# The position bias of the compressed keys and the latent products in the selector stage of a two-block transformer kernel

## What is computed

```python
# compressed keys (i=0) and values (i=1): blocks of 32 tokens, every 16, a learned position pe added to each
blocks = k[:, idx] + pe[:, None, :]
flat   = ....reshape(b, g, n_cmp, CMP_LEN * dh)          # 31 blocks, 2048 long
hid    = jax.nn.gelu(flat @ w1 + b1);  kc = hid @ w2 + b2
p_c    = softmax(q @ kc * scale)                          # per head: 512 x 31
# latent attention: keys and values per head from one latent row of 128 per token
sc     = (q_lat @ c_kv + q_rope @ k_rope) * scale ;  o = (p @ c_kv) @ w_uv
```

## Time and profile before

| | |
|---|---|
| median of 3 runs | 2381.52 us (2379.24 to 2383.43) |
| the profiled execution | 2381.52 us, span 2379.7 us |
| TensorE busy | 2275.6 us, 96% of the span |
| VectorE busy | 1028.7 us, 43% |
| ScalarE busy | 492.4 us, 21% |
| the stage `selector` | 232.7 to 350.4 us: 117.7 us |
| in it: TensorE, VectorE, ScalarE busy | 111.0, 96.7, 43.0 us |

### The profile page before, as it was taken

How to read it: one execution, slowest core, us unless ns; L and a number is a source line. 1 busy time by engine, 2 the same in 40 slices (tenths; PEclk the granted TensorE clock), 3 DMA queues, 4 the chain that set the end, 5 groups by cost and what they waited for, 6 DMA issues and landing times. The chain is left out here.

```text
span 2379.7 us, 26551 instructions
## 1 busy us (share of the span) xinstructions
PE 2275.6 (96%) x10439; PEld 1760.2 (74%) x10439; DVE 1028.7 (43%) x1931; ACT 492.4 (21%) x1131; POOL 687.0 (29%) x549
## 2 busy tenths in 40 slices
PE   7999988999999999999899999997999899999998
PEld 3454666677757888888778888884556568888887
DVE  4546965453335742254544223542623422111354
ACT  3101332223433000010400011112133532000002
POOL 0000000000010655565255555520010104555652
PEclk9999899899999999999999999998999999999999
DMA  9543334544431454222334432230122122232230
GB/s 322 181 134 103 112 107 142 177 155 112 106 103 39 149 185 127 81 77 73 106 125 159 142 95 70 77 110 31 36 76 71 36 71 71 71 106 60 74 97 36
DMA packets 255288, 250.14 MB, mean 105 GB/s; under 512 B 19875, under 2 KB 207421, under 8 KB 255037
## 3 DMA queue, kind: packets, MB, share of 16 engines
q1 hardware_dynamic: 254728, 248.30, 33.1%
q10 hardware_dynamic: 436, 0.15, 0.0%
HBM read 243.19 MB, written 4.19 MB: 104 GB/s over the span
## 5 line engine op out<-in xcount | busy, mean ns | idle before, releaser
L1985 POOL TENSOR_TENSOR w_sums<-ring 128x512 f32<-128x512 f32 x66 | 90.8, 1376 | 515.5 <-POOLq L1316 334.3
L2011 POOL TENSOR_TENSOR hidden<-rstd,h_act 128x256 f32<-128x256 f32 x66 | 53.8, 816 | 401.8 <-DVE h_act L2187 401.8
L1870 PE MATMUL ps<-h_sums,w_sums 128*128 128x256 f32 x528 | 128.4, 384 | 6.5 <-DVE h_sums L2123 6.1
L2187 DVE TENSOR_TENSOR h_act<-ps,rstd 128x256 f32<-128x256 f32 x78 | 33.1, 424 | 232.5 <-PE ps L1888 135.9
L814 PE MATMUL ps<-h_act,ring 128*128 128x512 f32 (+1 forms) x288 | 128.3, 600 | 5.2 <-PEq L333 4.4
L1888 PE MATMUL ps<-h_sums,ring 128*128 128x256 f32 x528 | 125.8, 381 | 3.1 <-DVE rstd L2166 3.0
L1876 PE MATMUL ps<-h_act,ring 128*128 128x256 f32 x528 | 126.4, 383 | 0.0
L1882 PE MATMUL ps<-h_sums,w_sums 128*128 128x256 f32 x528 | 125.0, 380 | 1.0 <-DVE rstd L2159 1.0
L1836 PE MATMUL ps<-h_act,ring 128*128 128x256 f32 x528 | 125.3, 381 | 0.0
L1893 PE MATMUL ps<-h_act,w_sums 128*128 128x256 f32 x528 | 124.8, 379 | 0.0
L1844 PE MATMUL ps<-h_act,ring 128*128 128x256 f32 x528 | 124.5, 380 | 0.0
(11 more groups left out here) (465 smaller groups left out, 4453.2 us busy)
## 6 DMA issues: line engine op xcount, KB each, us to landing
ring<-in_ffn_w_in SPq DMA_DIRECT2D x66, 1024.0 KB, 7.7
ring<-in_w_ada SPq DMA_DIRECT2D x12, 2048.0 KB, 9.1
ring<-in_w_mod SPq DMA_DIRECT2D x12, 2048.0 KB, 7.9
ring<-in_w_gate_up SPq DMA_DIRECT2D x22, 1024.0 KB, 8.2
ring<-in_ffn_w_out SPq DMA_DIRECT2D x32, 704.0 KB, 6.3
ring<-in_w_in SPq DMA_DIRECT2D x6, 2048.0 KB, 8.1
ring<-in_ffn_w_out SPq DMA_DIRECT2D x8, 1408.0 KB, 7.1
ring<-in_w_down SPq DMA_DIRECT2D x16, 704.0 KB, 6.0
```

Source lines behind the costliest of these rows:

```text
L1870: last = pe.matmul(pb, s2[:, k], F.t2[:, k], start=(k == 0), stop=(k == 3))
L1985: pool.tensor_tensor(s1, a21, a22, ALU.add).then_inc(S["wsum"].sem, 1)
L2011: pool.tensor_tensor(one[:, j], F.gate1[f % 2], F.got21[f % 2], ALU.mult)
L2187: dve.tensor_tensor(out21, pc, F.v, ALU.add).then_inc(S["got21"].sem, 1)
```

## The change

Two things change in `selector`.

The sum of `pe @ w1` leaves VectorE. Instead, TensorE multiplies each slice of `w1` by the matching column of `cmp_pe` and adds in PSUM: 16 products of one column for each i, where there was one. The contexts around them are spread: three between the columns, one after, where four stood after the one product.

The latent products move ahead of `prob_scores(0)` and `prob_scores(1)`, use four banks (2, 5, 3, 4) in place of two, and have no contexts between them; `context(8)` and a wait for all eight copies follow, then the two `prob_scores`, then `context(40)` in place of `context(32)`. The number of contexts in the stage stays 128.

```diff
-    pesum = K.sem("lc_pesum")
+    free = (2, 5, 3, 4)
...
-                pe.wait_ge(pesum, 31 + i)
-                pe.matmul(K.ps[3 + i][:, 64:65], M.cstd[:, P * i:P * i + P], K.ones[:, 0:1], start=True,
-                          stop=True).then_inc(hidm, 1)
-                context(4)
+                for m in range(16):
+                    last = pe.matmul(K.ps[3 + i][:, 64:65], w[:, i, m, :], K.p("cmp_pe", 16 * i + m, 1),
+                                     start=(m == 0), stop=(m == 15))
+                    if m % 4 == 3 and m < 15:
+                        context(1)
+                last.then_inc(hidm, 1)
+                context(1)
...
             pe.wait_ge(rel, 24)
-            pe.wait_ge(cmk, 2)
+            for j in range(4):
+                if j == 2:
+                    pe.wait_ge(cmk, 2)
+                pe.matmul(K.ps[free[j]][:, :], M.wuk[:, 2 * j:2 * j + 2, :], M.cT[:, :], start=True, stop=False)
+                pe.matmul(K.ps[free[j]][:, :], const(K, "esel", ROPE), M.kr[:, :], start=False,
+                          stop=True).then_inc(kvm, 1)
+            for t in range(QT):
+                pe.wait_ge(kvk, t + 1)
+                pe.matmul(K.ps[free[t]][:, :], M.cT[:, t * P:t * P + P], M.wuv[:, :, :].rearrange("p h d -> p (h d)"),
+                          start=True, stop=True).then_inc(kvm, 1)
+            context(8)
+            pe.wait_ge(kvk, 4 + QT)
             prob_scores(0)
             prob_scores(1)
-            for n in range(4 + QT):
-                if n >= 2:
-                    pe.wait_ge(kvk, n - 1)
-                dst = K.ps[n % 2][:, :]
...
-                last.then_inc(kvm, 1)
-                context(2)
-            context(32)
-            pe.wait_ge(kvk, 4 + QT)
+            context(40)
             prob_turn(0)
...
-                act.activation(dst, K.ps[n % 2][:, :], ACT.Copy).then_inc(kvk, 1)
+                act.activation(dst, K.ps[free[n % 4]][:, :], ACT.Copy).then_inc(kvk, 1)
...
-            w = K.ring.take(dve, "cmp").rearrange("p (i m h) -> p i m h", i=2, m=16)
-            for m in range(16):
-                for i in range(2):
-                    part, at = M.cstd[:, P * i:P * i + P], K.p("cmp_pe", 16 * i + m, 1)
...
-                        ins = dve.scalar_tensor_tensor(part, w[:, i, m, :], at, part, ALU.mult, ALU.add)
-                    else:
-                        ins = dve.tensor_scalar(part, w[:, i, m, :], at, None, ALU.mult)
-                    ins.then_inc(pesum, 1)
```

More of the change, by code:

```diff
@@ L1050, in _ @@
             pe.wait_ge(rel, 24)
-            pe.wait_ge(cmk, 2)
+            for j in range(4):
[10 more added lines that the diff above has]
+            pe.wait_ge(kvk, 4 + QT)
             prob_scores(0)
             prob_scores(1)
-            for n in range(4 + QT):
-                if n >= 2:
-                    pe.wait_ge(kvk, n - 1)
-                dst = K.ps[n % 2][:, :]
-                if n < 4:
-                    pe.matmul(dst, M.wuk[:, 2 * n:2 * n + 2, :], M.cT[:, :], start=True, stop=False)
-                    last = pe.matmul(dst, const(K, "esel", ROPE), M.kr[:, :], start=False, stop=True)
-                else:
-                    t = n - 4
-                    last = pe.matmul(dst, M.cT[:, t * P:t * P + P], M.wuv[:, :, :].rearrange("p h d -> p (h d)"),
-                                     start=True, stop=True)
-                last.then_inc(kvm, 1)
-                context(2)
-            context(32)
-            pe.wait_ge(kvk, 4 + QT)
+            context(40)
             prob_turn(0)
@@ L1241, in _ @@
                                          M.gkv[:, :], ALU.mult, ALU.mult).then_inc(nrm, 1)
-            w = K.ring.take(dve, "cmp").rearrange("p (i m h) -> p i m h", i=2, m=16)
-            for m in range(16):
-                for i in range(2):
-                    part, at = M.cstd[:, P * i:P * i + P], K.p("cmp_pe", 16 * i + m, 1)
-                    if m:
-                        dve.wait_ge(pesum, 2 * m - 1 + i)
-                        ins = dve.scalar_tensor_tensor(part, w[:, i, m, :], at, part, ALU.mult, ALU.add)
-                    else:
-                        ins = dve.tensor_scalar(part, w[:, i, m, :], at, None, ALU.mult)
-                    ins.then_inc(pesum, 1)
             for r in (1, 2):
```

## The result

The changed kernel took 2393.95 us (median of 4 runs, 2389.05 to 2395.77) against 2380.58 us (4 runs) for the kernel before beside it: ratio 1.0051, 95% interval 1.0032 to 1.0070. It is slower by 8 to 17 us. Forecast were 2383.9 us and no change that can be measured; the time lies above the range. In a second series, with more runs, the same kernel gave 1.0045 (1.0031 to 1.0060).

The account below looks back on a forecast made before the run. TensorE, busy 96%, was taken to bound the kernel, its 96th context product setting the stage's end. Columns +6.7, wait +1.3, latent block −9.8 and loop clock +4.15 gave +2.35 on 2381.5: 2383.9 us, range 2376 to 2391.

Parts of the forecast that it names:

- 30 columns more: In both compress loops: 30 more one-column products on TensorE cost 6.7 us, lower bound 4.2 us.
- wait for the hidden layer: After compress(1)'s last column: three contexts moved ahead no longer cover TensorE's wait for hidd, costing 1.3 us.
- half clock at the column loops and the wait: Around both column loops: one 3.4 us stretch (1.7 us) and one of 6.8 us (2.45 us) cost 4.15 us.
- latent block: First latent product to first value product: the new order gives back the half clock's whole cost, 9.84 us.
- 96th context product: Stream product that sets the stage's end: moves by −1.8 us, plus 4.15 us of loop clock, +2.35 us.
- the first stretch: After the first column loop: half clock for 3.4 us, costing 1.7 us.
- The slower rival: In the latent keys: half clock reaches them, 6.9 us lost again, 2390.8 us; chance 0.28.
- VectorE's saving: Before weigh(1): 8.3 us of instructions removed, 7.7 us remain, worth nothing because they end waiting for the exponentials.
- the third rival: At divide(0): the VectorE saving counts, 7.7 us come through, 2373.8 us; chance 0.12.
- no fall: In the column loops: lower bound for the half clock's cost, 0 us.
- the first rival: In the column loops: the clock holds, 2379.7 us, or 2377.2 us with cheap columns; chance 0.18.
- The fourth rival: At the moved prob_scores: clock falls again for one stretch, 1.7 us, 2385.6 us; counted within the forecast's spread.

Follow-up runs that it names:

- spread columns: Changed kernel with each one-column product right behind the 62-column product of the same slice, a context after every second slice: 2386.28 us, ratio 1.0031.
- one-column kernel: Changed kernel with only the last of the 16 column products for each i, leaving out 15 slices of the bias: 2377.52 us, ratio 0.9987.
- only the scores moved: Kernel before with prob_scores(0) and (1) put behind the latent products, two banks and context(2) after each kept: 2375.22 us, ratio 0.9974.
- the order alone: Changed kernel with the sum of pe @ w1 back on VectorE, new order of the latent products kept: 2378.39 us, ratio 0.9988.
- GpSimd kernel: Changed kernel's order with the sum of pe @ w1 on GpSimd, one TensorE product adding up the partitions: 2378.68 us, ratio 0.9998.
- before again: Kernel before, unchanged, run once more for a second profile: 2379.75 us against the series' 2382.08 us; the profiled execution took 2377.08 us.
- the columns alone: Changed kernel with the latent block as in the kernel before, column products still on TensorE: 2390.18 us, ratio 1.0039.
- grouped forms: New order, sum on VectorE, four wuk products then four esel; the second also has exponentials ahead of context_silu(5): 2378.57 and 2377.98 us, ratios 0.9990, 0.9992.

## Why the prediction failed

All times in us, later than before is plus.

| step | forecast | measured |
|---|---|---|
| 30 columns more | +6.7 | +6.70 (spread columns less one column) |
| wait for the hidden layer | +1.3 | +1.30 (one-column kernel) |
| half clock at the column loops and the wait | +4.15 | +5.8 (3.25 up to the product behind the hidden layer, 2.55 behind it) |
| latent block | −9.84 | −5.24 |
| 96th context product | +2.3 | +8.47 |
| span | +2.4 | +8.0 |

The two terms of issue and waiting hold to a tenth, and the loops' clock is short by 1.65 us. The latent block is short by 4.6 us, the largest miss. The 5.8 is worked out so: from the start of `compress(0)` to the product behind the hidden layer the changed kernel takes 33.88 us, less 30.63 for the spread columns; from there to the latent block 16.13 us in place of 13.58. Of these 2.55 us, 1.68 come without bunched columns too (the one-column and the spread kernel take 15.26 and 15.27 us there), behind the longer wait for the hidden layer; 0.87, with the 3.25 in all 4.1 us, come only with the bunched columns. The forecast had 1.7 us for the first stretch, which lasted 6.8 us where 3.4 were taken, and 2.45 for the second.

**The step that failed** is "The half clock cost 20.18 − 10.34 = 9.84 us" and "I count the 9.8 us as gained". At a clock of 1.00 it takes 31.85 us from the first latent product to the end of the 96th context product, in the order of the change (one-column and spread kernel) and with only the scores moved (three profiles). Before's own order, in which the same work starts with `prob_scores(0)`, was never seen at 1.00. Three things were wrong in the step.
- The price, 1.30 us. Before took 40.39, so the half clock cost 8.54 us, not 9.84. The forecast counted 0.86 us for each product, from a value product with a context behind it; the keys in the old order take 11.98 us at 1.00, not 10.34, because `wuk` and `esel` in turn are 1.05 us apart. That is no clock and could not come back.
- The clock in the new place, 3.30 us. The changed kernel takes 35.15 us there, 3.30 over the 31.85: the clock falls anew at 301.4, in the last pair of the latent keys. It did so with the order alone (287.7) and in the changed kernel's second profile (301.9), not in the one-column, the spread and the GpSimd kernel with the same order; in the last a stretch of 3.4 us came behind `prob_scores` instead (1.7 us). So the new order gets 8.54 − 3.30 = 5.24 us, the measured gain. The three kernels with only the scores moved had no fall in the block.
- The base. The 17.1 us of half clock stand in one execution. The old order stands in two more profiles, with 6.8 us (before again) and 10.2 us (the columns alone), where the way to the 96th product takes 35.45 and 37.14 us. So the half clock cost 8.5, 3.6 and 5.3 us, and the one price that the forecast had was the highest of the three.

The first two, with the 1.65 us of the loops, account for the 6.1 us by which the 96th product came later than forecast, and so for the profiled execution, 5.9 us over the forecast. The changed kernel's median is another 4.2 us above that execution, and no profile shows where they went; before's medians in four series, 2379.4 to 2382.08 us, lie around its profiled 2381.52.

The slower rival ("the half clock reaches the latent keys", 2390.8) has the nearest time, by luck and not by the way in which it came: the clock was back before the first `wuk` product (1.00 at 285), as the forecast had it, and fell anew in the block.

**What held.** VectorE's saving is worth nothing: the third rival is out, with 13.0 and 8.5 us of waiting. TensorE idles 1.64 us ahead of L1042, forecast 1.9. Columns are paced 0.203 us within four and 0.225 with what the next context then loses. The clock falls in the first column loop and behind the second, which was the choice between "no fall" and the falls of the earlier trace rows, and the first rival is out: the fall at 253.7 came with TensorE busy. Bunched one-column products are the cause in the first loop, since with one column, or with the columns between wider products, the clock stays at 1.00 there. The fall behind the second loop is not theirs alone, since those two kernels have a shorter one behind the same wait. The fourth rival's fall at the moved `prob_scores` came in the GpSimd kernel and not in the changed one, whose windows view has:

```profile
315.00:316.00 1.00, 1.00 (x16) 0.99 (x14) 0.70 (x3) 0.97 (x6) 0.00 (x0) 1.00 0.63 172
```

**Left open:** why the same order gives 6.8 us of half clock in one execution and 17.1 in the other, and what keeps the clock up in the latent block when only the scores move; the contexts between the products differ, and the two banks, but the one-column, the spread and the GpSimd kernel had neither and kept it up there too. Each of them has one profile, so chance is not ruled out.

## What to carry to other kernels

Work moved to the engine that is busy 96% costs its full issue time, however little it computes: 30 columns cost 6.7 us, and bunched another 4.1 us of clock; the contexts moved ahead of a wait no longer covered it, which cost 1.3 us and, by the clock, 1.7 us more. Look for a wait on the other engine before you move work off it (VectorE had 2.9 us of one). Price a lost clock against the same products at full clock, not against others, and from more than one execution, since the length of a stretch changes between them. The clock fell behind the narrow products in all three profiles with the old order; moving just these behind the wide ones brought more (0.26%) than rebuilding the block (0.12% in another series, and 0.10% and 0.08% for its grouped forms in the same series).

## What the runs showed of the hardware

- The clock fell with TensorE busy: among the one-column products at 253.7 and among 512-column products at 301.4. With the same one-column products put between 62-column ones it stayed at 1.00 through both loops (246 to 277).
- It also fell behind 1.64 us of idle time, at 270.1 and 279.0, for 3.4 us (one-column and spread kernel); with 0.34 us of idle time in the same place, before and with the order alone, it did not.
- Products with 128-row and 16-row weights in turn are 1.055 us apart, four of one kind together 0.907 us.
- VectorE's 128x128 instructions with two inputs went from 1.14 to 5.50 us for four while GpSimd worked.
- The same stretch of the same kernel ran at half clock for 17.1 us in one execution and for 6.8 us in another; with the columns ahead of it, 10.2 us.
